# A transformer layer with differential attention and a gated recurrence: early operand loads at one stage border, and who runs what, and when, inside the attention stage

## The reference, cut to what matters

```
h = rms_norm(x);  proj = h @ w_in      -> q, k, v (attention) | q, f, i, g (recurrence)
A: 4 heads; s1, s2 = q1 k1^T, q2 k2^T with a block-causal mask (chunks of 64), softmax each
   w = p1 - lam * p2;  o = rms_norm(w @ v) * 0.2
B: 4 heads, gated linear recurrence by chunks: S = diag(f) S + k v^T, o = S^T q,
   o = rms_norm(o) * silu(g)
x = x + concat(A, B) @ w_out;  x = x + SwiGLU(rms_norm(x)) @ w_down      all float32
```

## Time and profile before

| | |
|---|---|
| median of 3 runs | 2837.99 us (2837.49 to 2838.94) |
| profiled execution | 2841.29 us, its span 2839.6 us |
| PE busy | 2648.0 us, 93% |
| DVE, ACT, POOL busy | 54%, 38%, 27% |
| mean granted PE clock | 0.977 |

### The profile page before, as it was taken

One profiled execution on the slowest core, in us unless ns is written; L12 is line 12 of the kernel. 1 busy time (PEld: TensorE's weight loads), 2 busy tenths in 40 slices (PEclk: granted clock), 3 DMA queues, 4 the chain that ended last, 5 costly groups with the idle time before them and its releaser, 6 DMA issues. The chain is left out here.

```text
span 2839.6 us, 34056 instructions
## 1 busy us (share of the span) xinstructions
PE 2648.0 (93%) x13384; PEld 2239.5 (79%) x13384; DVE 1530.7 (54%) x1903; ACT 1086.8 (38%) x1807; POOL 773.6 (27%) x527
## 2 busy tenths in 40 slices
PE   7999999995998989896995999998999997999999
PEld 6888888885888888885884888887888886888887
DVE  5434343422676767672346666657566564456653
ACT  4434343331565656564334222224222221432321
POOL 5000000002434241500003444545445452145400
PEclk9999999997999999998997999999999998999999
DMA  4545455456343433205565333335333333787763
GB/s 160 196 163 179 143 185 175 134 178 177 88 103 97 111 90 97 75 1 193 178 223 207 98 102 105 101 112 185 107 102 100 112 99 93 247 296 256 252 215 125
DMA packets 338671, 415.78 MB, mean 146 GB/s; under 512 B 18512, under 2 KB 212048, under 8 KB 336720
## 3 DMA queue, kind: packets, MB, share of 16 engines
q1 hardware_dynamic: 338512, 413.60, 46.5%
HBM read 291.38 MB, written 122.16 MB: 146 GB/s over the span
## 5 line engine op out<-in xcount | busy, mean ns | idle before, releaser
L1824 PE MATMUL gate_bank<-gate_b_hi,gate_a_hi 128*128 128x512 f32 x1232 | 482.7, 392 | 38.4 <-DVE first_b_lo L1704 22.1
L1826 PE MATMUL gate_bank<-gate_b_hi,gate_a_lo 128*128 128x512 f32 x1232 | 481.7, 391 | 0.0
L1825 PE MATMUL gate_bank<-gate_b_lo,gate_a_hi 128*128 128x512 f32 x1056 | 412.8, 391 | 0.0
L1824 PEld LDWEIGHTS gate_bank<-gate_b_hi,gate_a_hi 128*128 128x128 f32 x1232 | 233.1, 189 | 88.9 <-issue 23.1
L1826 PEld LDWEIGHTS gate_bank<-gate_b_hi,gate_a_lo 128*128 128x128 f32 x1232 | 232.9, 189 | 48.8
L525 PE MATMUL proj_prod<-proj_w_hi,proj_h_hi 128*128 128x512 f32 x640 | 253.3, 396 | 6.8 <-DVE proj_w_lo L380 6.0
L2102 PE MATMUL down_prod<-down_w_hi,down_f_hi 128*128 128x512 f32 x616 | 241.3, 392 | 19.2 <-DVE down_f_lo L2038 18.3
L380 DVE TENSOR_TENSOR proj_w_lo<-proj_w_raw,proj_w_hi 128x2048 fp32r<-128x2048 f32 x56 | 128.4, 2294 | 230.3 <-ACT proj_w_hi L280 230.3
L527 PE MATMUL proj_prod<-proj_w_hi,proj_h_lo 128*128 128x512 f32 x640 | 250.4, 391 | 0.0
L526 PE MATMUL proj_prod<-proj_w_lo,proj_h_hi 128*128 128x512 f32 x640 | 250.1, 391 | 0.0
L2103 PE MATMUL down_prod<-down_w_lo,down_f_hi 128*128 128x512 f32 x616 | 240.8, 391 | 0.0
(11 more groups left out here) (212 smaller groups left out, 5581.0 us busy)
## 6 DMA issues: line engine op xcount, KB each, us to landing
proj_w_raw<-in_w_in_dram SPq DMA_DIRECT2D x56, 1024.0 KB, 6.4
first_full<-in_w_gate_dram SPq DMA_DIRECT2D x88, 256.0 KB, 4.0
gate_full<-in_w_up_dram SPq DMA_DIRECT2D x88, 256.0 KB, 4.0
ff<-gate_ff_sum SPq DMA_DIRECT2D x88, 256.0 KB, 2.9
down_w_raw<-in_w_down_dram SPq DMA_DIRECT2D x22, 1024.0 KB, 7.8
down_f_raw<-ff SPq DMA_DIRECT2D x56, 384.0 KB, 3.3
down_f_raw<-ff SPq DMA_DIRECT2D x56, 320.0 KB, 3.7
gate_b_lo<-operands SPq DMA_DIRECT2D x12, 1024.0 KB, 10.0
```

Source lines behind the costliest of these rows:

```text
L1824: pe.matmul(dst, a_hi[:, pos, s, :], b_hi[pos][:, s, :], start=opens and s == 0, stop=False, skip_group_check=True)
L1825: pe.matmul(dst, a_hi[:, pos, s, :], b_lo[pos][:, s, :], start=False, stop=False, skip_group_check=True)
L1826: last = pe.matmul(dst, a_lo[:, pos, s, :], b_hi[pos][:, s, :], start=False, stop=s == HALF_SLABS - 1, skip_group_check=True)
```

## The change

1. Operands of the first attention step live in tiles that exist in both stages (`First`). SP loads them in the last block of the projection, at unit 4 (`load_early`), into tiles of their own, and the first k and q of the recurrence into the tile that held x (`shared`).
2. The last v group is stored by tile, four DMAs (`store_last`).
3. POOL makes the next head's `whole` products ahead of the gate; six of the seven stand behind the last level. The update of side 0 of a level waits for the combination that DVE makes in the same step, and the gate (but in the last head) for the combination of step 14.
4. The normalising of the recurrence's chunks goes from DVE (one instruction a chunk) to ACT (four a chunk). After the last head ACT goes chunk by chunk.
5. In steps with three weight groups the second `weigh`, too, is put off into the next step, behind its first scores.

```diff
+            def store_last():
+                gi = GROUPS - 1
+                for t in range(SUB):
+                    sp.wait_ge(tile_read, gi * SUB + t + 1)
+                    row = (BLOCKS - 1) * TB + t * P
+                    sp.dma_start(out["v"][row:row + P, :], stage[gi % 2][0][:, t, :]).then_inc(stored[gi % 2], 16)
+            def load_early():
+                for par in range(2):
+                    sp.wait_ge(stored[par], stores_before(len(ORDER) + (len(ORDER) + par) % 2))
+                tokens = slice(0, TB)
+                load_keys(sp, out, 0, tokens, early.k, early.k_in)
+                load_queries(sp, out, 0, tokens, early.q_hl, early.q_lh, early.q_in)
+                load_features(sp, out["hf"], 0, early.rf[:], early.rf_in)
...
+                sp.wait_ge(slab_turned, (BLOCKS - 1) * KS)
+                load_features(sp, out["hk"], 0, early.rows(1), early.rqk_in)
+                load_features(sp, out["hq"], 0, early.rows(0), early.rqk_in)
...
+                if b == BLOCKS - 1 and u == 4:
+                    load_early()
+            store_last()
...
+    def behind(s):
+        return 1 if groups_of(s) == 3 else 2
...
+            def behind_combination(h, n):
+                step = h * STEPS + n // 2
+                if n % 2 == 0 and step:
+                    pool.wait_ge(combined, step)
+            def gate(h):
+                pool.wait_ge(rgate_in, 16 * (h + 1))
+                pool.wait_ge(fill_read, filled(h, len(FILLS) - 1))
+                if h + 1 < HEADS:
+                    pool.wait_ge(combined, (h + 1) * STEPS - 1)
+                nc.gpsimd.tensor_tensor(ro[:], ro[:], rgate[:], ALU.mult).then_inc(r_gated, 1)
...
+                        n = fill_at("level", side, m)
+                        pool.wait_ge(fill_done, filled(h, n))
+                        behind_combination(h, n)
...
+                if h + 1 < HEADS:
...
+                    pool.wait_ge(rf_in, 16 * (h + 2))
+                    for m in range(LEVELS - 1):
+                        product(h + 1, m)
+                    pool.wait_ge(fill_read, filled(h, len(FILLS) - 1))
+                    product(h + 1, LEVELS - 1)
+                gate(h)
...
(scalar)
+                    act.wait_ge(r_rrms_made, h + 1)
+                    act.wait_ge(r_gated, h + 1)
+                    head = c - TURNS
+                    for t in range(CH):
+                        part = ro[:, t, head * C:(head + 1) * C]
+                        at = t * HEADS + head
+                        nc.scalar.activation(part, part, ACT.Copy, scale=ro_rrms[:, at:at + 1]).then_inc(r_scaled, 1)
...
                 for head, c in chunks_at(s):
+                    if s == TOTAL + 1 and c + 1 < CHUNKS:
+                        normalise(head, c + 1)
                     take_chunk(head, c)
...
(tensor)
-                    for g in range(2, groups_of(s - 2)):
+                    for g in range(behind(s - 2), groups_of(s - 2)):
                         weigh(s - 2, g)
...
-                    if g < 2:
+                    if g < behind(s - 1):
                         weigh(s - 1, g)
```

More of the change, by code:

```diff
@@ L117, in make_level_masks, with __init__, rows, head_rows @@
         steps += 4
-def project(nc, x, attn_g, w_in, q_g, k_g, ident, pair_sel, eps, out, masks):
+class First:
+    def __init__(self, a, landed):
+        self.k_in, self.q_in, self.rf_in, self.rqk_in, self.small_in = landed
+        self.shared = a.sb("shared", [P, 2, HEADS * TB])
+        self.q_hl, self.q_lh, self.k = (a.sb(n, [P, 2, TB], F32R) for n in ("q_hl", "q_lh", "k"))
+        self.rf = a.sb("rf", [P, HEADS, TB])
+        self.lams = a.sb("lams", [P, 4, DH])
+        self.g_col, self.rg_col = a.sb("g_col", [P, 1]), a.sb("rg_col", [P, 1])
+    def rows(self, t):
+        return self.shared[:, t, :].rearrange("p (h n) -> p h n", n=TB)
+def head_rows(scratch, h, base, tokens):
+    return scratch[h * P + base:h * P + base + P, tokens].rearrange("(m p) n -> p m n", p=DH)
+def load_queries(sp, mid, h, tokens, q_hl, q_lh, sem):
+    for tile, names in ((q_hl, ("qk_hi", "qk_lo")), (q_lh, ("qk_lo", "qk_hi"))):
+        for part, name in zip((slice(0, DH), slice(DH, P)), names):
+            sp.dma_start(tile[part].bitcast(F32), head_rows(mid[name], h, 0, tokens)).then_inc(sem, 16)
+def load_keys(sp, mid, h, tokens, dst, sem):
+    for part, name in ((slice(0, DH), "qk_hi"), (slice(DH, P), "qk_lo")):
+        sp.dma_start(dst[part].bitcast(F32), head_rows(mid[name], h, W, tokens)).then_inc(sem, 16)
+def load_features(sp, scratch, b, dst, sem):
+    sp.dma_start(dst, scratch[:, b * TB:(b + 1) * TB].rearrange("(h p) n -> p h n", p=P)).then_inc(sem, 16)
+def project(nc, x, attn_g, w_in, q_g, k_g, ident, pair_sel, eps, out, masks, early, lambdas, subln_g, hgrn_g):
     KH = KS // 2
@@ L211, in destinations, with stores_of @@
                     HI: lambda: [tokens("hv")], HG: lambda: [tokens("hgate")]}[kind(gi)]()
+        def stores_of(gi):
+            return SUB if gi == GROUPS - 1 else len(destinations(gi))
         def stores_before(gi):
-            return sum(16 * len(destinations(m)) for m in range(gi % 2, gi, 2))
+            return sum(16 * stores_of(m) for m in range(gi % 2, gi, 2))
         def rooted(nb):
@@ L655, in mix_tokens @@
         r = Alloc(nc, ctx, "rec")
-        rq, rk, rf = (r.sb(n, [P, HEADS, TB]) for n in ("q", "k", "f"))
+        rq, rk, rf = early.rows(0), early.rows(1), early.rf
         rv, rgate = (r.sb(n, [P, CH, W]) for n in ("v", "gate"))
@@ L695, in mix_tokens @@
         stored = [a.sem(f"stored{b}") for b in range(STAGES)]
-        rf_in, rqk_in, rv_in, rgate_in = (r.sem(n) for n in ("f_in", "qk_in", "v_in", "gate_in"))
+        rf_in, rqk_in = early.rf_in, early.rqk_in
+        rv_in, rgate_in = (r.sem(n) for n in ("v_in", "gate_in"))
         whole_made = r.sem("whole_made")
@@ L1046, in _ @@
                     invert_roots(h - 1)
-                for head, c in chunks_at(s + 1) if s <= TOTAL - 1 else chunks_at(s):
-                    normalise(head, c)
         @block.tensor
@@ L1064, in score @@
                         if k + wide == (j + 1) * P:
-                            pe.matmul(ring[:, at + wide - P:at + wide], early[:], late[:], start=False, stop=False, skip_group_check=True)
+                            pe.matmul(ring[:, at + wide - P:at + wide], early_rows[:], late_keys[:], start=False, stop=False, skip_group_check=True)
                         last = pe.matmul(dst, q_lh[b][:, m, q], keys, start=False, stop=True)
```

129 lines of the change are left out of this document (54 added, 75 removed).

## The result

The changed kernel takes 2788.75 us (2787.56 to 2789.98, 4 runs); the kernel before, on the same chip, 2838.47 (2837.49 to 2840.85, 4 runs): ratio 0.9824 [0.9807, 0.9841]. The profiled execution has a span of 2786.9 us instead of 2839.6, so 52.7 us less, where 43.6 were forecast.

What follows compares the result with a forecast made beforehand. PE was taken to lose time at the border into attention and in recurring attention-stage waits, one followed by a lower clock. Terms summed to -43.6 us, from 2838.0 to 2794.4; bounds together 2784 to 2806, with rivals 2784 to 2811.

Steps and rivals of the forecast that it cites:

- The border: From projection to attention: smaller last store and early loads bring the second fill sooner, -22.0 us, bounds 16 to 24.
- The early loads: In the projection: unit 49's weights leave about 5 us late, PE's cover holds; 0, bounds 0 and +4 us.
- Step 5: Steps 5 and 6, heads 1 to 3: normalising on ACT ends PE's wait and the clock's fall; -12.5 us, bounds 6 and 15.
- Collisions, steps 7 and 8: POOL's update started behind DVE's combination no longer lengthens it; -5.0 us over four heads, bounds 2 and 6.
- Step 15: Heads 0 to 2: products moved and gate held back end PE's wait of 1.27 us; -3.9 us, bounds 1 and 4.
- The products' new place: Step 9, three heads: POOL's products and DVE's combination block each other; +1.2 us, bounds 0 and 3.
- The second weigh: Steps 10 to 13: put off behind the next first scores, it fills PE's waits; -6.0 us, 1.5 a head.
- Behind the last head: After the last head ACT alone normalises and takes the chunks, with nothing hiding it; +4.6 us, bounds 3 and 6.
- Late v: Rival at the border: v lands up to 6 us behind its use, border gives only 16; 2800 us, chance 0.12.
- ACT in DVE's place: Rival, steps 4 to 6: exponentials stand behind ACT's 16 activations, 12.5 and 6.0 us lost; 2813 us, chance 0.10.
- POOL's hold: Rival "slower": PE waits for POOL's side 0 updates held behind the combination, clock falls; about 2894 us, chance 0.03.

Runs made afterwards that it cites:

- one store: The changed kernel with the last block's v stored as one 1 MB DMA again: 2792.15 us, ratio 0.9833.
- POOL's order of before: The changed kernel with POOL's gate first, then the seven products, and no wait for the combination: 2800.16 us, ratio 0.9859.
- the two kernels built on that one: Changed kernel, DVE normalising behind the last head, second weigh put off in steps 6 to 13: 2772.24 us; the same with steps 4 to 15: 2770.49.

## Why the prediction was right, point by point

The mechanisms held but for one, and nearly every gain came out larger than its term: 51.2 us against 43.6, spread over the border (2.1), step 5 (2.3), steps 7 and 8 (0.7), step 15 (1.7) and the last head (0.9).

The working has one fault in the range: the terms' bounds, added at their best, give 2784.8, but at their worst 2826 and not 2806, so its upper end took it that not all would go wrong at once.

**The border.** Right, at its bound of 24. The step that was mis-sized is the store by tile: 1.5 by the estimate, 2.3 to 2.5 at the stage's start, and with it the clock rises sooner, so that the run with one store loses 3.4 by the medians. The order of what is late next was right: the masks, then DVE's row; v was never late.

**The early loads.** Right in the outcome, wrong in the working: the weights left 9.4 us later, not 5, since the fifteen DMAs took 20 us to issue there and not 15. PE's 9 us of cover held with ACT's wait of 3.5 inside it.

**Step 5.** The size was right (14.8 for 12.5), the cause half. I gave the whole wait of 2.10 to DVE's normalising. The runs show two contributions, 2.70 us of normalising and 1.63 of POOL's updates, and that taking away either one alone is enough: with DVE normalising but POOL held, steps 5 and 6 lose 0.7 a head; with POOL not held but ACT normalising, nothing. The clock only falls when both are there. ACT's price of 0.3 a head was nothing.

**Collisions, steps 7 and 8.** Right in mechanism and size, 5.7 for 5.0; by the run without the hold it is this wait alone that gives it. The rule of an exclusive port pair, from the Trainium skill's page "SBUF — State Buffer", in its part on the two separate sides, is borne out a second time: with the hold undone, the 896-column combination goes from 1.15 back to 2.01.

**Step 15.** Right in mechanism, 5.6 for 3.9: the next step's 0.35 was left out. It comes from the products' place, not from the gate's hold.

**The products' new place.** The combination there does grow, 1.86 for 1.42. But PE stands for exponentials then, not for the combination: 0.05 us in each of three heads instead of +1.2.

**The second weigh.** Mis-sized: 1.5 a head forecast, 1.97 measured, or -7.9 in all. And one step was missing: I looked for a fall of the clock at no place but step 5. In step 9 PE's wait of 2.29 us, which stood there before as well and cost no clock in any head, now does in heads 1 and 2, and that took 3.0 us back. So forecast and measurement of this row meet by luck. What had changed around that wait is PE's work: the put-off weigh of step 8, eight passes with v, left step 9 for step 10.

**Behind the last head.** Right: 16.5 us of ACT for 17.4, +3.7 for +4.6, and the run with DVE there gives 3.4 of it back.

**The rivals.** Late v did not come (no wait of PE for v). ACT in DVE's place did not either, though ACT is busy for 8.9 of 10 us in steps 5 and 6 and the first exponentials of step 5 come 1.5 us later behind the start of the step than before: PE has other work until then. POOL's hold delays nobody.

## What to carry to other kernels

When a wait is to be removed, list all that makes its releaser late, and ask whether one of them alone is enough: two edits at one wait aren't worth the sum of their prices. Give every wait of two microseconds a price for the clock as well: here the same 2.29 us cost another 1.5 in some heads and not in others, and the cure was to put the engine's own work into it. Work that nothing waits for yet (here a product with v) belongs behind the instructions that another engine waits for, and each step that has such a wait is a place for it.

## What the runs showed of the hardware that I had not expected

- A wait of one length may cost the clock or not. In step 9 PE waits 2.29 us in every head of all rows but the last, and another 0.3 at the step's end in most heads where the second weigh is put off. Its length by head is:

| | head 0 | 1 | 2 | 3 |
|---|---|---|---|---|
| kernel before | 8.83 | 8.85 | 8.83 | 8.83 |
| changed kernel | 8.57 | 10.05 | 10.00 | 8.52 |
| DVE behind the last head | 8.57 | 10.05 | 10.06 | 9.89 |
| one store | 8.57 | 9.94 | 8.57 | 9.97 |
| chunks normalised by DVE | 8.57 | 8.57 | 8.57 | 9.94 |
| early loads put back | 9.92 | 8.57 | 9.97 | 10.06 |
| POOL's order of before | 9.50 | 8.53 | 8.51 | 9.82 |
| hold alone undone | 9.58 | 9.93 | 9.59 | 10.04 |
| second weigh in its old place | 8.92 | 8.92 | 10.39 | 8.85 |
| put off in steps 6 to 13 (wait 1.40) | 8.77 | 8.77 | 8.78 | 8.51 |

With one store, all behind the border runs some 4 us later and is otherwise the same program; head 2 is short then, and head 3 long. With a wait of 1.40 no head is long, and none is in the two kernels built on that one. The Trainium skill's page "TensorE: Matmul & The Clock Gate", Part 1, says that the monitor isn't synchronised with the kernel and that the number of slow passes at a start differs from run to run; the table agrees, and shows the same for a fall in mid-kernel. But chance need not be all: with the weigh of step 8 in step 9 (the kernel before, and the second weigh in its old place) 1 head of 8 is long, without it 17 of 28. Each row is one profiled execution, so how much of the loss belongs to the put-off weigh is not shown.
- POOL blocks even DVE's smallest operation with SBUF inputs: a 128x1 instruction took 1.06 us instead of 0.22 when an update of POOL had begun 0.05 us ahead of it.
- A store's size shows at a barrier with its full time: 2.46 us from issue to the next stage's first load with 256 KB, 4.75 with 1 MB.
